# A hybrid encoder step on one core: another order in the attention loops, a 128-row own block, a shorter router and 22 unread products

## What is computed

```python
def block_attention(q, k, v, ...):        # per head
    s = einsum('bqhd,bkhd->bhqk', qi, k) * scale   # FoX: + bias_q - bias_k
    p = softmax(where(visible, s, -inf), axis=-1)
    return einsum('bhqk,bkhd->bqhd', p, v)

def moe(x, router_w, router_bias, w_gate, w_up, w_down):
    scores = sigmoid(x @ router_w)
    grouped = (scores + router_bias).reshape(B, T, 4, 4)
    group_score = sum(top_k(grouped, 2)[0], axis=-1)
    best = argmax(group_score)                       # one group of four experts
    masked = where(in_group, grouped, -inf)
    _, idx = top_k(masked, 2)                        # two experts of it
    w = scores[idx] / sum(scores[idx])
    y = sum over e of (silu(x @ w_gate[e]) * (x @ w_up[e])) @ w_down[e] * combine[e]
```

## Time and profile before

| | us |
|---|---|
| median of 3 runs | 1240.25 (1239.88 to 1240.64) |
| profiled execution | 1235.15 |
| its span | 1233.1 |
| TensorE busy in the span | 1119.4 (91%), mean granted clock 0.97 |
| VectorE / ScalarE / GpSimd busy | 559.4 / 254.0 / 222.4 |
| FoX loop | about 309 to 361 |
| MLA loops | about 772 to 830 and 865 to 923 |
| router, logits to mask, layer 0 / layer 1 | 440.8 to 449.5 / 1006.8 to 1015.5 |

### The profile page before, as it was taken

One profiled execution on the slowest core, in us unless ns is written; L12 is line 12 of the kernel. 1 busy time (PEld: TensorE's weight loads), 2 busy tenths in 40 slices (PEclk: granted clock), 3 DMA queues, 4 the chain that ended last, 5 costly groups with the idle time before them and its releaser, 6 DMA issues.

```text
span 1233.1 us, 18806 instructions
## 1 busy us (share of the span) xinstructions
PE 1119.4 (91%) x7327; PEld 623.0 (51%) x7332; DVE 559.4 (45%) x1346; ACT 254.0 (21%) x610; POOL 222.4 (18%) x382
## 2 busy tenths in 40 slices
PE   8999999999889979999949989999999988999965
PEld 4556777554664633333315546776774553333312
DVE  2079879610643353744357140440442354554336
ACT  1214245321420000111101122332320000111112
POOL 0106445420201110101044210000000111100114
PEclk9999999999899989999989999999999989999987
DMA  8103302261734186999766222001205175899835
GB/s 355 69 9 141 125 33 105 86 226 65 44 130 175 52 345 246 339 413 375 281 214 222 70 106 69 1 1 68 69 8 231 62 298 209 329 397 407 316 103 196
DMA packets 41974, 215.54 MB, mean 175 GB/s; under 512 B 4504, under 2 KB 6104, under 8 KB 32544
## 3 DMA queue, kind: packets, MB, share of 16 engines
q1 hardware_dynamic: 24432, 153.28, 31.8%
q0 software_dynamic: 17168, 60.27, 15.8%
q10 hardware_dynamic: 288, 0.80, 0.2%
HBM read 181.02 MB, written 33.29 MB: 174 GB/s over the span
## 4 chain that ended last, share of the span: by engine, by line
PE 78%; DVE 9%; issue 4%; DMA 3%; ACT 3%; POOL 1%; DVEq 0%; SPq 0%; ACTq 0%
PE pair L1516 12%; PE pair L1131 9%; PE pair L1410 9%; PE pair L1537 7%; PE pair L1252 5%; PE pair L1330 5%; PE pair L1614 5%; PE pair L1142 4%; PE pair L1374 3%; PE pair L1119 2%; PE pair L1502 2%; PE pair L1372 2%; DMA ring<-in_even_w_in 2%; DMA arena<-x_rows,ints 1%; PE pair L1647 1%
## 5 line engine op out<-in xcount | busy, mean ns | idle before, releaser
L1516 PE MATMUL pair<-ring,arena 128*32 128x512 f32 x608 | 128.5, 595 | 0.0
L1131 PE MATMUL pair<-ring,xT 128*128 128x512 f32 x256 | 111.3, 593 | 0.9 <-DMA ring<-in_even_w_in 0.9
L1516 PE MATMUL pair<-arena 128*32 128x512 f32 x736 | 100.5, 600 | 8.0 <-issue 4.5
L1252 PE MATMUL pair<-xT,ring 128*128 128x296 f32 x320 | 85.1, 421 | 6.9 <-ACT arena L1726 3.0
L883 POOL TENSOR_SCALAR small<-small 128x1 f32<-128x1 f32 (+3 forms) x45 | 15.2, 337 | 386.9 <-DVE small L2264 334.5
L905 POOL TENSOR_TENSOR arena<-arena 128x128 f32<-128x128 f32 x140 | 58.4, 451 | 145.5 <-PE pair L1178 78.9
L1131 PEld LDWEIGHTS pair<-ring,xT 128*128 128x128 f32 x256 | 48.1, 190 | 59.7 <-issue 57.9
L1330 PE MATMUL pair<-arena 128*128 128x264 f32 (+8 forms) x270 | 74.6, 407 | 2.8 <-ACT arena L1716 1.8
L1031 POOL DMA_INDIRECT arena<-x_rows,ints x26 | 26.4, 1014 | 264.9 <-PE pair L1502 163.4
L1252 PEld LDWEIGHTS pair<-xT,ring 128*128 128x128 f32 x320 | 60.4, 193 | 25.8 <-issue 9.3
L2402 DVE COPY arena<-pair 128x256 f32<-128x256 f32 x26 | 11.0, 423 | 135.4 <-PE pair L1525 135.4
(11 more groups left out here) (385 smaller groups left out, 1968.1 us busy)
## 6 DMA issues: line engine op xcount, KB each, us to landing
arena<-in_moe_w_gate_up SPq DMA_DIRECT2D x14, 2048.0 KB, 8.8
ring<-in_moe_w_gate_up SPq DMA_DIRECT2D x12, 2048.0 KB, 9.4
arena<-in_moe_w_down SPq DMA_DIRECT2D x14, 1024.0 KB, 9.2
y_rows<-arena SPq DMA_DIRECT2D x26, 512.0 KB, 8.5
ring<-in_moe_w_down SPq DMA_DIRECT2D x12, 1024.0 KB, 11.3
xT<-in_moe_w_gate_up SPq DMA_DIRECT2D x6, 2048.0 KB, 14.6
ring<-in_even_w_in SPq DMA_DIRECT2D x5, 2048.0 KB, 7.9
y_rows<-xr POOLq DMA_DIRECT2D x12, 512.0 KB, 8.5
```

The source lines that it names most:

```text
L1131: last = pe.matmul(ps[0:P, 0:n], xT[:, k, 128 * i:128 * i + P], w[:, k, :], start=(k == 0), stop=(k == chunks - 1))
L1252: last = pe.matmul(ps[0:w.shape[2], 512 * s:512 * s + n], w[:, k, :], xT[:, k, n * s:n * s + n], start=(k == 0), stop=(k == KD - 1))
L1516: last = pe.matmul(bank[c, :], xgT[:, e % 2, k, c], expert_place(x)[0][:, k, :], start=(k == 0), stop=(k == KD - 1))
```

## The change

In `attention` TensorE has the transposes of n-2 before the values of n-3, and VectorE has maximum, scaling, own, out. For "pair" units the own block is 128 columns of the probabilities, the 64 own ones and the first 64 of the past, against `cvp`: 64 rows of latents and 64 of zeros, written once. The router finds the best two of each group of four as the largest of three sums, masks the groups with one fused operation, multiplies both choices by `valid` at once, and writes the bf16 mask straight from the last sum; the float mask follows it. The first `keep_busy` has 22 products.

```diff
--- before.py
+++ after.py
@@ -288,6 +288,7 @@
         kpst = r2.take(4 * 128).rearrange("p (j n) -> p j n", j=4)
         qrd = r3.take(4 * 128).rearrange("p (k s) -> p k s", k=4)
         qrm = r3.take(MH * NM)
+        cvp = r3.take(KVL)
         assert max(r2.n, r3.n) <= ARENA - ATT
 
         rtmp = arena[:, ARENA - 1024:ARENA].rearrange("p (b n) -> p b n", b=4)
@@ -336,7 +337,6 @@
         lg = col(NT * NE).rearrange("p (i e) -> p i e", i=NT)
         sc_ = col(NT * NE).rearrange("p (i e) -> p i e", i=NT)
         mk = col(NT * NE).rearrange("p (i e) -> p i e", i=NT)
-        sel1 = col(NT * NE).rearrange("p (i e) -> p i e", i=NT)
         gs = col(NT * 4).rearrange("p (i e) -> p i e", i=NT)
         gs2 = col(NT * 4).rearrange("p (i e) -> p i e", i=NT)
         t5a, t5b = col(NT), col(NT)
@@ -731,7 +731,7 @@
 
             kind, _, i = att_units[n]
             if kind == "pair":
-                return slice(NM, 80), slice(0, NS)
+                return slice(NM, NM + 128), slice(0, 128)
             if kind == "meta":
                 return slice(NS, 80), slice(NS, 80)
             R = TILES[4] if i == 4 else 128
@@ -1366,7 +1366,8 @@
                     values = [(mv_[rows, 4, hc], [mv_[:, j, hc] for j in range(nb)])]
                 else:
                     outs.append(psum[pair_of[("PT", n)]][:, 384:512])
-                    values = [(cvo[rows, 128 * c:128 * c + 128], [ckpv[:, j, 128 * c:128 * c + 128] for j in range(nb)])
+                    own = cvp if kind == "pair" else cvo
+                    values = [(own[rows, 128 * c:128 * c + 128], [ckpv[:, j, 128 * c:128 * c + 128] for j in range(nb)])
                               for c in range(2)]
                 for out, (vo, vb) in zip(outs, values):
                     last = pe.matmul(out, vo, pT[rows, n % 2, 512:512 + P], start=True, stop=(nb == 0))
@@ -1378,10 +1379,10 @@
                 for n in range(first, last + 3):
                     if n < last:
                         att_scores(n)
+                    if first <= n - 2 < last:
+                        att_transpose(n - 2)
                     if n - 3 >= first:
                         att_values(n - 3)
-                    if first <= n - 2 < last:
-                        att_transpose(n - 2)
 
             pe.wait_ge(*lf_sb["x"])
             pe.wait_ge(*fq_sb[3])
@@ -1418,7 +1419,7 @@
 
                 for i in (NT - 2, NT - 1):
                     pe.wait_ge(*ps_free[("wo", l, i)])
-                keep_busy(30)
+                keep_busy(22)
                 pe.wait_ge(*mk_sb[l])
                 ps = claim(pe, ("rk", l))
                 for i in range(NT):
@@ -2215,12 +2216,12 @@
                 for n in range(first, last + 3):
                     if n < last:
                         att_max(n)
+                    if first <= n - 1 < last:
+                        att_scale(n - 1)
+                    if first <= n - 2 < last:
+                        att_own(n - 2)
                     if n - 3 >= first:
                         att_out(n - 3)
-                    if first <= n - 2 < last:
-                        att_own(n - 2)
-                    if first <= n - 1 < last:
-                        att_scale(n - 1)
 
             def pad_probs():
 
@@ -2269,6 +2270,7 @@
                 stt(r, r, lrs[0:P, b, 1:2], lng[0:P, 1, :], ALU.mult, ALU.add).then_inc(r_sb.sem, 1)
 
             R = [rtile(n) for n in range(10)]
+            chosen = RW[:, 3 * 80:5 * 80].rearrange("p (c i e) -> p c i e", c=2, i=NT)
             f80 = lambda v: v.rearrange("p i e -> p (i e)")
             over_i = lambda v: v.unsqueeze(1).to_broadcast([128, NT, v.shape[1]])
 
@@ -2283,26 +2285,23 @@
                 q = n20(R[0])
 
                 tt(S[1], q[:, :, 0], q[:, :, 1], ALU.max)
-                tt(S[2], q[:, :, 0], q[:, :, 1], ALU.min)
-                tt(S[3], q[:, :, 2], q[:, :, 3], ALU.max)
-                chain(tt(S[4], q[:, :, 2], q[:, :, 3], ALU.min))
-                tt(S[5], S[1], S[3], ALU.max)
-                tt(S[6], S[1], S[3], ALU.min)
-                chain(tt(S[7], S[2], S[4], ALU.max))
-                chain(tt(S[6], S[6], S[7], ALU.max))
+                tt(S[3], q[:, :, 0], q[:, :, 1], ALU.add)
+                tt(S[2], q[:, :, 2], q[:, :, 3], ALU.max)
+                chain(tt(S[4], q[:, :, 2], q[:, :, 3], ALU.add))
+                tt(S[5], S[1], S[2], ALU.add)
+                chain(tt(S[6], S[3], S[4], ALU.max))
                 g = gs.rearrange("p i e -> p (i e)")
-                chain(tt(g, S[5], S[6], ALU.add))
+                chain(tt(g, S[5], S[6], ALU.max))
 
                 chain(dve.tensor_reduce(t5a, gs, AX, ALU.max))
                 chain(tt(gs2, gs, bc(t5a, 4), ALU.is_equal))
                 chain(tt(gs2, gs2, over_i(const("prio4")), ALU.mult))
                 chain(dve.tensor_reduce(t5b, gs2, AX, ALU.max))
-                chain(tt(gs2, gs2, bc(t5b, 4), ALU.is_equal))
-                chain(tt(n20(R[1]), q, bc(gs2.rearrange("p i e -> p (i e)"), 4), ALU.mult))
-                chain(ts(gs2, gs2, -NEG, NEG, ALU.mult, ALU.add))
-                chain(tt(n20(R[1]), n20(R[1]), bc(gs2.rearrange("p i e -> p (i e)"), 4), ALU.add))
-                for c, sel in ((0, sel1), (1, mk)):
-
+                chain(tt(gs2, gs2, bc(t5b, 4), ALU.is_lt))
+                chain(stt(n20(R[1]), bc(gs2.rearrange("p i e -> p (i e)"), 4), NEG, q, ALU.mult, ALU.add))
+                for c in range(2):
+
+                    sel = chosen[:, c]
                     chain(dve.tensor_reduce(t5a, R[1], AX, ALU.max))
                     chain(tt(R[2], R[1], bc(t5a, NE), ALU.is_equal))
                     chain(tt(R[2], R[2], over_i(const("prio16")), ALU.mult))
@@ -2310,10 +2309,9 @@
                     chain(tt(sel, R[2], bc(t5b, NE), ALU.is_equal))
                     if c == 0:
                         chain(stt(f80(R[1]), f80(sel), 2 * NEG, f80(R[1]), ALU.mult, ALU.add))
-                    chain(tt(sel, sel, bc(const("valid"), NE), ALU.mult))
-                chain(copy(R[4], mk))
-                chain(tt(mk, mk, sel1, ALU.add))
-                copy(maskb[:, :], f80(mk)).then_inc(mk_sb.sem, 1)
+                chain(tt(chosen, chosen, const("valid").unsqueeze(1).unsqueeze(3).to_broadcast([128, 2, NT, NE]), ALU.mult))
+                tt(maskb.rearrange("p (i e) -> p i e", i=NT), chosen[:, 0], chosen[:, 1], ALU.add).then_inc(mk_sb.sem, 1)
+                chain(tt(mk, chosen[:, 0], chosen[:, 1], ALU.add))
 
                 key = ("rk", l)
                 ps = filled(dve, key)
@@ -2327,9 +2325,9 @@
 
             def slots_and_weights(l):
 
-                for c, sel in ((0, sel1), (1, R[4])):
-                    chain(tt(R[3], sel, sc_, ALU.mult))
-                    chain(dve.tensor_reduce(wts[:, c, :], R[3], AX, ALU.add))
+                for c in range(2):
+                    chain(tt(R[8], chosen[:, c], sc_, ALU.mult))
+                    chain(dve.tensor_reduce(wts[:, c, :], R[8], AX, ALU.add))
                 chain(tt(t5a, wts[:, 0, :], wts[:, 1, :], ALU.add))
                 chain(ts(t5a, t5a, 1e-37, None, ALU.max))
                 chain(dve.reciprocal(t5a, t5a))
@@ -2349,8 +2347,8 @@
                 chain(tt(R[7], R[6], over_i(ovn), ALU.mult))
                 chain(tt(R[7], R[7], over_i(cnt), ALU.add))
                 chain(tt(R[7], R[7], R[5], ALU.add))
-                for c, sel in ((0, sel1), (1, R[4])):
-                    chain(tt(R[8], R[7], sel, ALU.mult))
+                for c in range(2):
+                    chain(tt(R[8], R[7], chosen[:, c], ALU.mult))
                     chain(dve.tensor_reduce(posf[:, c, :], R[8], AX, ALU.add))
                 chain(copy(posi, posf))
 
@@ -2579,6 +2577,8 @@
             dve.wait_ge(*pe_full[("pt", 3)])
             dve.memset(qrd, 0.0)
             dve.memset(qrm, 0.0).then_inc(pez_sb.sem, 1)
+            dve.memset(cvp[NS:128, :], 0.0)
+            copy(cvp[0:NS, :], cvo[0:NS, :])
             pad_probs()
             for g in range(2):
                 key = ("qa", g)
```

## The result

The changed kernel takes 1224.53 us (median of four, 1222.95 to 1226.83) against 1240.07 for the kernel before in the same comparison: ratio 0.987, 95% interval 0.9844 to 0.9896. That is 15.5 us less between the medians, and 16.1 by the ratio (12.9 to 19.3). Forecast were 10.7 us less; the measured median lies at the lowest edge of the forecast range of 1224.5 to 1236, and by the ratio just past it.

The account below looks back on a forecast made before the run. TensorE carries 78% of the chain, so only its stalls or own work count. Attention order 6.1, deep own block 1.7 and router 2.9 sum to 10.7 us: median 1240.25 becomes 1229.5, range 1224.5 to 1236.

Parts of the forecast that it names:

- rival (a): Attention loops: the waits only change hands and attention gains 0, giving 1235.6 us; chance 0.20.
- carry the difference to the median unchanged: Sum against the profiled execution, 1235.15 us, and keep its distance to the timed median, 1240.25, the same after the change.
- attention order, FoX (steady and end): FoX loop: the wait per head shrinks by 0.51, 2.0 us over four heads; the loop's end gains 1.1.
- attention order, MLA (heads and two ends): Two MLA loops: one wait a head shrinks, 0.8 us in all; each loop's end gains 1.1.
- deep own block: Four pair units: a 128-row own block saves 0.42 us a unit, 1.7 in all.
- router, up to the mask: VectorE's chain from logits to mask shortens by 1.45 us a layer, 2.9 for two layers.
- runs eight of them in 1.06; a pair unit needs 0.42 and 1.16: Value products: a full unit's 0.31 and 1.06 against a pair unit's, 0.21 us lost for each of two column halves.
- The upper bound of 2.2: Deep own block: at most 2.2 us, counting the 0.09 by which the first product starts late.
- four savings: Router on VectorE, per layer: stage one 0.30, group masking 0.48, valid product 0.20, last add writing bf16 0.47 us.
- a cover of 2.2 us: Layer 0 behind the mask: first gather lands at 458.1, unread products end at 460.30, so TensorE ends the stage.
- a sign of being wrong: The prediction called itself wrong if the stage behind the mask ends on the gather.
- rival (d): Router: path not shortened because the gather lands later among the weights; 2.9 us less gain, 1232.4; chance 0.07.

## Why the prediction was right or wrong, step by step

**Sign and mechanism** were right: the wait changed hands and shrank, and rival (a), nothing gained in attention, is out. **The size was not**: 10.7 forecast, 15.5 measured. Two terms of the sum were too small, by 2.3 to 2.5 us together, and the step "carry the difference to the median unchanged" failed by 4.6.

| term | forecast | measured by lengths |
|---|---|---|
| attention order, FoX (steady and end) | 2.0 + 1.1 | 3.2 |
| attention order, MLA (heads and two ends) | 0.8 + 2.2 | 4.15 |
| deep own block | 1.7 | 2.8 to 3.0 |
| router, up to the mask | 2.9 | 3.0 |
| sum | 10.7 | 13.2 to 13.4 |
| not assigned | 0 | 2.2 of the 15.5 between medians; 2.8 and 3.4 by the two ratios |

- **FoX** holds: new wait 0.59 printed for 0.6, head period 11.62 to 11.01 or 11.02, two waits at the end (0.89 and 0.48) for three.
- **MLA order is the first mis-sized term**, 1.15 too small. The six waits of the first loop (printed 3.71 in sum) became five (2.60), by issue slots 1.27 less, where the forecast's 0.4 + 1.1 a loop had 1.5. What was left out is a second effect: right behind the mask an own product takes 0.31 to its successor (786.80 to 787.11), behind T only 0.22 (786.41 to 786.63). The weight loads (PEld) tell the two apart. Before, the load of the own product starts 0.03 ahead of it (786.77), since the mask product of 64 columns in front takes no longer to the next start; in the changed kernel it starts 0.11 ahead (786.30). That the mask is bf16 is not what counts: in the FoX loop of before an own product stands behind a bf16 mask of 512 columns, its load starts 0.22 ahead (317.58), and it takes 0.22 too. An own product behind a wait, whose load starts with it, takes 0.33. T right behind a mask or a wait goes on in 0.14 instead of 0.11. The net is 0.06 to 0.08 for each of 14 units in the first loop (8 right behind the mask, 6 behind a wait), some 0.85. The forecast gave only waits a price, and moved products none. The rows (the first and the last four from before, the second from the changed kernel):

```profile
786.77 0.30 PEld L1372 LDWEIGHTS pair<-arena 128*128 128x128 f32 x2
...
786.30 0.30 PEld L1373 LDWEIGHTS pair<-arena 128*128 128x128 f32 x2
...
317.58 0.38 PE L1335 MATMUL pair<-cstb,identb 80*80 80x512 bf16 x1
317.58 0.41 PEld L1372 LDWEIGHTS pair<-arena 128*128 128x128 f32 x2 [0.31 <-issue]
317.80 0.38 PE L1372 MATMUL pair<-arena 128*128 128x128 f32 x2
...
318.02 0.61 PE L1374 MATMUL pair<-arena 128*128 128x128 f32 x4
```

- **Deep own block is the second**, 1.1 to 1.3 too small. The failed step is "runs eight of them in 1.06; a pair unit needs 0.42 and 1.16". The printed busy times end at modelled ends; by start times the way out of the 64-row unit's past products is dearer too (1.09 for 0.89). The upper bound of 2.2 was made from the same rows and was too low for the same reason (and 1.7 with four times 0.09 gives 2.0, not 2.2).
- **Router** holds to 0.05 a layer, in each of its four savings. The 22 products end before the mask, with waits of 0.58 and 2.09 in the two profiles around the forecast 1.7; the difference is the clock at which they ran.
- **Behind the mask** the forecast had TensorE, not the gather, end the stage with a cover of 2.2 us. It took the gather's 4.6 us over from the kernel before, but beside more weights the gather takes 5.1 to 6.1, and the cover does not exist in every execution: in the second profile of the changed kernel the stage of layer 0 ends on the gather, which the forecast had named as a sign of being wrong. So rival (d) was right on the mechanism and wrong on the price: router and 22 products alone gained 3.3 us, not 0. The intervals allow for all of the 1.45 a layer or for a third of it.
- **The carried difference to the median failed.** Forecast was a median 5.1 above the profile as in before; in the changed kernel it is 0.5. The forecast of the profiled execution (1224.5 for 1224.0) came out through two errors that cancel: the terms were 2.5 to 2.7 too small, and the changed kernel's profile met 48.3 us of busy low clock where the first of before met 43.7, and half of the difference, 2.3, was lost. That it came out is luck.
- **The surplus** of 2.2 to 3.4 us over the stages is not explained. The clock was the first guess, rival (b)'s favourable case in other places than it named. For it speaks that TensorE's busy time at 1.2 GHz was 53.7 to 57.9 us in five of the six profiles that lack the new order on TensorE, on VectorE or on both (43.7 in the sixth), and 45.5 to 54.3 in the five with both orders and VectorE's scaling behind max; half of the difference of the medians (54.6 and 49.8) is 2.4. Against it speaks that single profiles of one kernel spread by more than that, and the timed executions show no change. The mean granted clock is 0.967 in the 26 and in the 15 executions of before timed beside these runs, and 0.967 in the 4 and 4 of the changed kernel, which makes 81 to 83 us at 1.2 GHz on average in all of them; the clock can explain the surplus only if these stretches fall on idle time more often, and no run isolates that. Another 0.4 of it lies outside the span: 1.8 us on average in the changed kernel, 2.2 and 2.3 in before. The rest may be noise: the 13.3 us of the stages lie inside the interval of the first comparison (12.9 to 19.3) and just below that of the second (13.9 to 19.7).

The parts alone measure 6.7 + 1.7 + 3.3 = 11.7 us by their ratios, less than the whole, 16.1 and 16.7 in two comparisons. Each part has an interval of about 2 us to either side, so their sum allows for the 13.3 of the stages. Whether the parts together hold something beyond the sum stays open.

## What to carry to other kernels

When engines that each keep their written order share a software pipeline, change the order on all of them as one: T ahead of V cost 9 us on TensorE alone, nothing was gained on VectorE alone, and both gave 7 less. Price an edit on TensorE by the distance of start times up to the next unchanged instruction, never by printed busy times, and give moved products a price as well as waits. A transfer asked for earlier can take longer, since it meets other traffic: read its landing again in the changed kernel. Take a second profile of the kernel before as the base, since one execution can lie 5 us beside its median, in this case with the difference where the clock was low.

## What the runs showed of the hardware

- A 64-row fp32 product among 128-row ones costs 0.09 to 0.20 us at each change, 0.70 to 0.75 us for a unit with two of them.
- A pair of fp32 products of 128 columns took 0.22 us to the next start where the first one's weight load starts 0.11 or 0.22 us ahead, 0.31 where it starts 0.03 ahead, and 0.33 where it starts with the product.
- The same indirect gather of 128 rows landed 4.4 to 4.9 us behind its issue with 0.15 to 0.6 MB on the other queue in its first 5 us, and 5.1 to 6.1 us with 0.8 to 1.3 MB.
- Dependent operations of VectorE on 20, 80 and 160 elements start 0.21, 0.275 and 0.36 us apart.
- Identical code met 43.7 and 57.3 us of busy time at 1.2 GHz in two executions, and took 1235.15 and 1240.83 us.
